# Delta rule in four groups: level masks applied by VectorE to the product P, both products of a level in two banks, and the next group's convolution inside this group's levels

## What is computed

```
proj = h @ w_in                                   # q, k (8 heads each), v, z (16 heads), width 128 each
qkv  = silu(causal_depthwise_conv(qkv, conv_w))   # 4 taps along time
q, k = l2norm(q) * 128**-0.5, l2norm(k)
decay  = exp(where(causal, gc_i - gc_j, -inf))    # gc: running sums of g
a_low  = where(strict, (k*beta) @ k.T * decay, 0)
t_inv  = inverse(eye + a_low)                     # lower triangular solve
u, w   = t_inv @ (v*beta), t_inv @ (k*beta*exp(gc))
v_new  = u - w @ state
o      = (q*exp(gc)) @ state + ((q @ k.T) * decay) @ v_new
state  = state*exp(g_last) + (k*exp(g_last-gc)).T @ v_new
out    = (rmsnorm(o) * silu(z)) @ w_o
```

## Time and profile before

| | before |
|---|---|
| median of 3 runs | 1782.59 us (1781.35 to 1784.86) |
| profiled execution, its own time | 1781.98 us |
| its span | 1780.2 us |
| PE busy | 1696.2 us, 95% |
| DVE / ACT / POOL busy | 1317.5 / 1062.6 / 177.9 us |
| DeltaNet groups in the trace | 359.7 to 735.1 us |

### The profile page before, as it was taken

The page is one execution under the profiler, slowest core; times in us unless marked ns, Lnnn a source line. Parts: engine busy times, 40 slices in busy tenths (PEclk is TensorE's granted clock), DMA queues, the critical chain, the costliest instruction groups (busy, mean ns, idle before and its releaser), DMA issues.

```text
span 1780.2 us, 23186 instructions
## 1 busy us (share of the span) xinstructions
PE 1696.2 (95%) x8998; PEld 1435.6 (81%) x8998; DVE 1317.5 (74%) x1065; ACT 1062.6 (60%) x1012; POOL 177.9 (10%) x118
## 2 busy tenths in 40 slices
PE   8899999889999988889999999999999999999996
PEld 6789998778888877768888888888888888888884
DVE  5644445494857655379889889899898898898986
ACT  4444343554545353266777777777777777777773
POOL 0100000044442617000000000000000000000000
PEclk9899999999999999989999999999999999999999
DMA  9146555242221200359999999999999999999992
GB/s 349 43 141 212 173 189 171 92 140 74 70 95 48 71 1 1 154 190 352 354 364 356 350 358 371 348 361 358 350 364 348 372 344 353 365 369 346 369 361 112
DMA packets 155422, 437.91 MB, mean 246 GB/s; under 512 B 9280, under 2 KB 40416, under 8 KB 155360
## 3 DMA queue, kind: packets, MB, share of 16 engines
q1 hardware_dynamic: 155360, 437.03, 68.3%
HBM read 435.95 MB, written 1.05 MB: 245 GB/s over the span
## 4 chain that ended last, share of the span: by engine, by line
PE 83%; DVE 10%; ACT 3%; issue 2%; DMA 1%; POOL 0%; SPq 0%; DVEq 0%; ACTq 0%; POOLq 0%
PE bank L1328 24%; PE bank L1330 24%; PE bank L1329 24%; DVE wlo L844 2%; PE bank L1708 2%; PE bank L1697 2%; PE bank L1810 1%; ACT whi L521 1%; DVE T L1097 1%; DVE TT L1119 1%; PE bank L1715 1%; DVE cvall L1036 1%; DMA raw<-in_attn_w_qkv_dram 1%; DVE wlo L1164 0%; PE bank L1833 0%
## 5 line engine op out<-in xcount | busy, mean ns | idle before, releaser
L1164 DVE TENSOR_TENSOR wlo<-raw,whi 128x2048 fp32r<-128x2048 f32 x336 | 767.6, 2291 | 111.9 <-ACT whi L745 108.8
L745 ACT CAST whi<-raw 128x2048 fp32r<-128x2048 f32 x336 | 643.4, 1916 | 245.3 <-PE bank L1330 245.3
L1328 PE MATMUL bank<-whi,xhi 128*128 128x512 f32 (+1 forms) x1584 | 576.9, 364 | 12.8 <-ACT oall L647 3.5
L1330 PE MATMUL bank<-whi,xlo 128*128 128x512 f32 (+1 forms) x1584 | 568.9, 359 | 0.0
L1329 PE MATMUL bank<-wlo,xhi 128*128 128x512 f32 (+1 forms) x1584 | 568.5, 359 | 0.0
L1328 PEld LDWEIGHTS bank<-whi,xhi 128*128 128x128 f32 x1584 | 301.1, 190 | 59.1 <-DVE wlo L844 4.1
L1330 PEld LDWEIGHTS bank<-whi,xlo 128*128 128x128 f32 x1584 | 300.9, 190 | 44.5
L1329 PEld LDWEIGHTS bank<-wlo,xhi 128*128 128x128 f32 x1584 | 301.4, 190 | 41.9
L844 DVE TENSOR_TENSOR wlo<-raw,whi 128x2048 fp32r<-128x2048 f32 x75 | 186.7, 2491 | 108.4 <-ACT whi L521 108.1
L1328 PE MATMUL bank<-whi,ehhi 128*128 128x512 f32 x448 | 178.3, 398 | 1.8 <-DVE ehlo L1179 1.8
L521 ACT CAST whi<-raw 128x2048 fp32r<-128x2048 f32 x75 | 142.9, 1905 | 60.2 <-PE bank L1330 56.0
(11 more groups left out here) (266 smaller groups left out, 1639.6 us busy)
## 6 DMA issues: line engine op xcount, KB each, us to landing
raw<-in_moe_w_gate_dram SPq DMA_DIRECT2D x112, 1024.0 KB, 6.8
raw<-in_moe_w_up_dram SPq DMA_DIRECT2D x112, 1024.0 KB, 6.8
raw<-in_moe_w_down_dram SPq DMA_DIRECT2D x112, 1024.0 KB, 6.9
raw<-in_dn_w_in_dram SPq DMA_DIRECT2D x24, 1024.0 KB, 5.3
raw<-in_ffn_w_gate_dram SPq DMA_DIRECT2D x11, 1024.0 KB, 5.8
raw<-in_ffn_w_up_dram SPq DMA_DIRECT2D x11, 1024.0 KB, 5.2
raw<-in_ffn_w_down_dram SPq DMA_DIRECT2D x11, 1024.0 KB, 4.9
raw<-in_dn_w_o_dram SPq DMA_DIRECT2D x8, 1024.0 KB, 5.2
```

The lines of the kernel that those rows point to most:

```text
L745: act.copy(slot(whi, n, SPLIT), slot(raw, n, RAW)).then_inc(hi_ready, 1)
L1164: dve.tensor_tensor(slot(wlo, n, SPLIT), slot(raw, n, RAW), slot(whi, n, SPLIT).bitcast(F32), ALU.subtract).then_inc(lo_ready, 1)
L1328: pe.matmul(ps, lhs_hi, wh, start=start, stop=False)
L1330: return pe.matmul(ps, lhs_lo, wh, start=False, stop=stop)
```

## The change

GpSimd no longer masks `A` (its 24 instructions of L473 go, `off0` and `off1` too). PE multiplies `A` itself with `TT`, and VectorE multiplies the level's mask, now transposed in the table, into P where it leaves its bank, in place of ScalarE's copy. The second product of a level and the transpose of `T` at the start go to banks 2 and 3 as well. Banks 4 and 5 so are free in the levels, and the convolution of group g+1 is done in the levels of group g: transposes in levels 1 and 4, VectorE's rounds one by one behind the subtractions, Silu in levels 4 and 6, and the decay sums behind w. Group 0's own convolution comes before the loop. `outputs_lo`, the second output block's norm and `add_outputs` move to other places of VectorE's stream; the tables of halves and panels are new (six halves ahead of the levels in groups 0 to 2, and 6, 10 and 10 in them); in group 3 two of four halves move into levels 1 and 2, and 12 activity matmuls stand for 19.

```diff
@@ scheduling tables
-        FILLED = ((2, 3, 4, 5, 6, 7, 7, 8, 9, 10, 11, 12, 12, 12), (2, 3, 4, 5, 6, 8, 9, 10, 11, 12, 13, 14, 15, 16),
-                  ..., (0, 0, 1, 2, 3, 4, 4, 4, 4, 4, 4, 4, 4, 4))
+        FILLED = ((2, 3, 4, 4, 5, 6, 7, 8, 9, 10, 11, 12), (2, 3, 4, 5, 6, 6, 8, 10, 11, 12, 14, 16),
+                  ..., (0, 0, 1, 2, 2, 2, 3, 4, 4, 4, 4, 4))
@@ gpsimd
-                pool.wait_ge(sem("A_ready"), g + 1)
-                off_diagonal(g, 1)
-                off_diagonal(g, 2)
                 scaled(g, 2, kbe, ebeta)
                 scaled(g, 2, ktail, etail)
-                for lv in range(3, LEVELS):
-                    off_diagonal(g, lv)
@@ scalar, in the levels
-                    for b in range(TB):
-                        act.wait_ge(sem("P_psum"), 2 * u + b + 1)
-                        act.copy(Pm[:, 4 * b:4 * b + 4, :], four(2 + b)).then_inc(sem("P_ready"), 1)
+                    if more and lv == 1:
+                        taps(g + 1, 0)
+                    if more and lv == 4:
+                        taps(g + 1, 1)
@@ vector, before the loop
+            for w in (2, 1, 0):
+                conv_round(0, 0, w)
             lo_panels.upto(LIST[0] + 1)
             z_scaled(0)
+            for w in (2, 1, 0):
+                conv_round(0, 1, w)
@@ vector, in the levels
+                    mask = tb_(f"level{lv}").unsqueeze(1).broadcast_to([P, GH, P])
+                    for b in range(TB):
+                        dve.wait_ge(sem("P_psum"), 2 * u + b + 1)
+                        dve.tensor_tensor(Pm[:, 4 * b:4 * b + 4, :], bank[2 + b]..., mask, ALU.mult)\
+                            .then_inc(sem("P_ready"), 1)
+                    ahead(lv)
+                    if more and lv == 6:
+                        z_scaled(g + 1)
                     for b in range(TB):
                         dve.wait_ge(sem("dTT_psum"), 2 * u + b + 1)
-                        dve.tensor_tensor(t_, t_, bank[4 + b]..., ALU.subtract)\
+                        dve.tensor_tensor(t_, t_, bank[2 + b]..., ALU.subtract)\
                             .then_inc(sem("TT_ready"), 1)
+                    if more and lv < 4:
+                        conv_round(g + 1, 0, 3 - lv)
...
@@ tensor, new functions
+            def conv_T(g, half):
+                pe.wait_ge(sem(("prj_qk_ready", "prj_v_ready")[half]), g + 1)
+                if half:
+                    pe.wait_ge(sem("conv_ready"), 2 * g + 1)
+                elif g:
+                    pe.wait_ge(sem("qdT_ready"), g)
+                ...
+            def decay_sums(g):
+                pe.wait_ge(sem("gm_ready"), g + 1)
+                pe.wait_ge(sem("conv_ready"), 2 * g + 2)
+                for b in range(TB):
+                    i = pe.matmul(bank[4 + b], tb_("ones"), gm[:, 4 * b:4 * b + 4, :], start=True, stop=True)
+                i.then_inc(sem("R_psum"), 1)
@@ tensor, before the loop
+                if i == 8:
+                    conv_T(0, 0)
+            conv_T(0, 1)
             pe.wait_ge(sem("gate_act"), 4)
+            decay_sums(0)
@@ tensor, levels and tail
-                            i = pe.matmul(bank[2 + b][...], o[:, 4 * b + h, :], TT[:, 4 * b + h, :],
+                            i = pe.matmul(bank[2 + b][...], A[:, 4 * b + h, :], TT[:, 4 * b + h, :],
                                           start=True, stop=True)
                         i.then_inc(sem("P_psum"), 1)
-                    filling(6 + lv)
+                    filling(5 + lv)
+                    if more and lv in (1, 4):
+                        conv_T(g + 1, lv // 4)
...
-                filling(13)
+                if more:
+                    decay_sums(g + 1)
```

More of the change, by code:

```diff
@@ L69, in table @@
         s = 1 << n
-        parts[f"level{n}"] = (i // (2 * s) == j // (2 * s)) & (i // s % 2 == 1) & (j // s % 2 == 0)
+        low, up = (i, j) if n == 0 else (j, i)
+        parts[f"level{n}"] = (low // (2 * s) == up // (2 * s)) & (low // s % 2 == 1) & (up // s % 2 == 0)
     at, out = 0, []
@@ L142, in trunk @@
     vb = eight("vb", 48)
-    qkT, off1 = eight("qkT", 52), eight("off1", 52)
+    qkT = eight("qkT", 52)
     A = eight("A", 56)
@@ L621, in _ @@
             act.wait_ge(sem("baT_psum"), 1)
-            act.copy(hid[0:2 * VH, 0:SEQ], bank[4][0:2 * VH, 0:SEQ]).then_inc(sem("baT_ready"), 1)
+            act.copy(hid[0:2 * VH, 0:SEQ], bank[2][0:2 * VH, 0:SEQ]).then_inc(sem("baT_ready"), 1)
             act.wait_ge(sem("rs_ready"), 3)
@@ L665, in ahead @@
                 def ahead(place):
[L666 to L673, removed]
+                    hi_panels.upto(LIST[g] + HI_AHEAD[g][place] - 1)
@@ L694, in _ @@
-                ahead(1)
                 act.wait_ge(sem("qkT_psum"), g + 1)
                 for b in range(TB):
-                    i = act.copy(qkT[:, 4 * b:4 * b + 4, :], four(b))
+                    i = act.copy(qkT[:, 4 * b:4 * b + 4, :], four(2 + b))
                 i.then_inc(sem("qkT_ready"), 1)
@@ L1110, in _ @@
                     dve.tensor_tensor(t_, eye, t_, ALU.subtract).then_inc(sem("T1_ready"), 1)
-                ahead(2)
+                if g:
+                    add_outputs(g - 1, 0, lambda b, h: 6 + b).then_inc(sem("outputs_added"), 1)
                 for lv in range(1, LEVELS):
                     u = g * (LEVELS - 1) + lv - 1
+                    mask = tb_(f"level{lv}").unsqueeze(1).broadcast_to([P, GH, P])
+                    for b in range(TB):
+                        dve.wait_ge(sem("P_psum"), 2 * u + b + 1)
+                        dve.tensor_tensor(Pm[:, 4 * b:4 * b + 4, :], bank[2 + b].rearrange("p (n f) -> p n f", n=4), mask, ALU.mult)\
+                            .then_inc(sem("P_ready"), 1)
+                    ahead(lv)
+                    if more and lv == 6:
+                        z_scaled(g + 1)
                     for b in range(TB):
@@ L1622, in filling @@
                     done[0] = max(done[0], FILLED[g][place])
-                for half in range(2):
-                    pe.wait_ge(sem(("prj_qk_ready", "prj_v_ready")[half]), g + 1)
-                    for t in range(4 * half, 4 * half + 4):
-                        src = (group_part(g), prj_v)[half]
-                        for b in range(TB):
-                            i = pe.transpose(conv_src(t)[:, b * P:(b + 1) * P], src[:, b, t % 4 * P:(t % 4 + 1) * P], ident)
-                    i.then_inc(sem("ch_psum"), 1)
+                if g:
+                    pe.wait_ge(sem("v_ready"), TB * g)
+                    pe.wait_ge(sem("S_ready"), g)
+                back(g, 0, 2)
                 filling(0)
-                if g == GROUPS - 1:
+                if not more:
                     pe.wait_ge(sem("z_scaled"), GROUPS)
-                    keep_clock(5, bank[6])
+                    keep_clock(12, bank[6])
                 if g:
```

259 lines of the change are left out of this document (128 added, 131 removed).

## The result

The changed kernel takes 1792.11 us (median of 5 runs, 1790.44 to 1793.61) against 1782.59: ratio 1.0050, 95% interval 1.0039 to 1.0061, 9.5 us slower. The forecast was 1785.1, its range ended at 1790.5. The profiled execution has a span of 1790.3 us, 10.1 over before. PE is busy 4 us more than before and GpSimd 77 less, with its masks gone.

The account below looks back on a forecast made before the run. PE, holding 83% of the chain, was taken as the bound, so only its waits count. Groups 0 to 3 gave 5.1 + 0.7 + 0.7 - 4.0 = +2.5 us, 1785.1 us; range 1777 to 1790.5.

Parts of the forecast that it names:

- Group 0, +5.1 forecast: First DeltaNet group, its own convolution ahead of the loop: ends at 457.5, 5.1 us later than before.
- The wait ahead of the decay sums: Group 0's start: PE idles 7.2 us, 360.8 to 368.0, until VectorE's convolution rounds end.
- the 2.3: Group 0's front: 2.3 us lost to the lower clock behind PE's idle stretch, taken from 1.7 or 3.0.
- Groups 1 and 2, +0.7 each forecast: Middle DeltaNet groups: front, levels and tail together 100.6 us against 99.9, 0.7 us more in each.
- the front at 26.6 us: Groups 1 and 2 ahead of the levels: 38.8 us less moved work is 25.9, plus 0.7 waiting for P.
- the pairs for `T` alone: Groups 1 and 2, VectorE's copies to `T` beside GpSimd: first pair 2.8 us, second 2.3; alone 1.4 each.
- the wait for the addition to `X`: Level 1 of groups 1 and 2: the half behind P waits 2.4 us for this addition on VectorE.
- Group 3, -4.0 forecast: Last DeltaNet group: level 3 starts at 43.4 us into the group instead of 47.4, 4.0 us less.
- my 1.5: Group 3's front: PE's 4.6 us idle stretch before `onlo` costs about 1.5 us more by the clock.
- Masks and banks at 0: All levels: VectorE's mask product adds 0 to 0.1 us a level, taken as 0; sharing one bank pair costs nothing.
- The first: Rival: clock falls at level 1 of groups 1 and 2, 1.7 us lost in each; +5.9, 1788.5; chance 0.23.
- The second: Rival: VectorE's copies to `T` wait a whole GpSimd instruction, 3.4 us a pair; +5.9, 1788.5; chance 0.12.

Follow-up runs that it names:

- a_lock: The changed kernel, but GpSimd's mask product of `E` waits until VectorE's panels ahead of `A` are made; 1788.6 us, ratio 1.0028 to the kernel before.
- a_lock2: The changed kernel, with GpSimd's mask product of `E` held until VectorE's panels are made (groups 0 to 2) and its scalings until `T` is made; 1783.9 us, ratio 1.0001.
- b_masks2: The kernel before with VectorE's level masks alone, convolution unmoved, each level's panel put between its mask and its subtraction; 1778.5 us, ratio 0.9974.
- a_clock: The changed kernel, with products of no use filling PE's four long idle stretches to hold the clock; 1789.3 us, ratio 1.0034 to the kernel before.

## Why the prediction was wrong, step by step

- **Group 0, +5.1 forecast, +6.5 measured.** The wait ahead of the decay sums was right (7.2 forecast, 6.92), and the clock fell behind it (the sums took 3.43 from start to start instead of 1.72, so 1.7 of the 2.3). P came 51.3 us behind the gate sums, where the forecast has 50.9 (397.2 against 346.26; its own terms add up to 397.0), although `A` was late by the collision (a_lock gave 1.2 back), so other terms were a little too large. In level 5 VectorE's subtraction stood behind a panel that started late since ScalarE's cast was (the row), and the level took 9.0 us instead of 7.8. So the levels took 49.5 us, not 48.3.
```profile
432.43 2.29 DVE L843 TENSOR_TENSOR wlo<-raw,whi 128x2048 fp32r<-128x2048 f32 x1 [2.31 <-ACT whi L511]
```
- **Groups 1 and 2, +0.7 each forecast, +2.4 measured.** This is the step that failed. I had the front at 26.6 us; it took 29.9. The sum took PE's moved work off before's front and added 0.7; it had no term for a wait of PE for VectorE's panel behind the transposes of q and k. I put GpSimd's collisions on the pairs for `T` alone (2.8 and 2.3), and they fell on the two panels ahead, 7.32 instead of 4.49. That cost PE 2.0 us of wait and 1.7 of clock; without them, in a_lock2, the front is 26.2. The pairs took 2.09 and 1.29. The levels took 60.5, not 62.1: the wait for the addition to `X` was 0.9, not 2.4, since the pair ahead of it ran alone. The tail was right, 11.9. Without the collision (a_lock2) these groups last 98.6, under my 100.6.
- **Group 3, -4.0 forecast, -1.3 measured.** PE did wait for `onlo`, 5.45 us instead of 4.6, and the clock stayed low for 6.9 us, where my 1.5 stands for some 3. The chain ahead was longer than summed: the reduction began 5.4 us into the group (4.9 forecast), and the scaling of q and k took 2.02 beside GpSimd's products for `EB`, against 1.23 before:
```profile
669.07 0.92 DVE L1078 TENSOR_SCALAR par<-par 128x4 f32<-128x4 f32 x1 [2.11 <-POOL par L438]
670.02 2.02 DVE L1079 TENSOR_TENSOR qk<-qk,par 128x1024 f32<-128x1024 f32 x1
671.97 1.28 DVE L1020 TENSOR_TENSOR onlo<-bank,onhi 128x512 fp32r<-128x512 f32 x2
```
  P came 28.4 us into the group, not 26.3, and level 3 at 45.6, not 43.4.
- **Masks and banks at 0: right for the masks where they stand; the bank pair has no run of its own.** All 48 mask products took 676 to 692 ns. A level without halves takes 5.17 us instead of 5.05 (705.94 to 711.11; the earlier trace rows), the 0.1 at the end of my range, and b_masks2 is faster than before with the same masks. I gave their removal from GpSimd and ScalarE no gain, and b_masks2 shows 4.5 us, with the panels' new place in the levels in it.
```profile
L1127 DVE TENSOR_TENSOR Pm<-bank,tabs x48: 676/691/692, 395.5 to 723.4; 128x512 f32<-128x512 f32 x48
```
```profile
705.94 1.95 PE L1721 MATMUL bank<-TT,A 128*128 128x128 f32 x16
...
711.11 1.06 PE L1721 MATMUL bank<-TT,A 128*128 128x128 f32 x8
```
- **The rivals.** The first (the clock falls at level 1 of groups 1 and 2) had the price right, 1.7 us a group, and the place wrong: it fell in the front, behind a wait that the rival doesn't have. In these groups it came at level 1 only in a_clock. The second (a whole instruction of GpSimd ahead of each of VectorE's) is what happened, on other instructions than I named. The Trainium skill (SBUF — State Buffer, SBUF: two separate sides) says that whichever starts first holds the shared port for its whole instruction; the trace agrees, since GpSimd's product began at 469.52 and the panel, begun at 469.76, ended 2.14 us after that product's end, close to the 2.28 that it takes alone.

## What to carry to other kernels

When work is moved away from an engine, list what its remaining instructions now stand beside, not only what they cost: here GpSimd's mask product came to stand beside two panels in a row, and its scalings, which no longer wait for `A`, right behind it. Two waits that hold early, unneeded instructions back until their neighbours are done lengthened nothing that PE needs and returned 8.7 us (1.0050 to 1.0001). Two causes in one chain can each give little alone (0.3 and 1.2 us, and 4.0 together): repair both before calling either useless.

## What the runs showed of the hardware

A VectorE instruction that reads a bank kept its length beside GpSimd. In the changed kernel no mask product stood beside it, but in a_lock2 the first ones of groups 0 to 2 did, and took 680 to 692 ns all the same:
```profile
482.84 2.04 POOL L466 TENSOR_TENSOR kbe<-qk,par 128x512 f32<-128x512 f32 x2 [6.96 <-DVE T L1123]
483.87 1.28 DVE L1131 TENSOR_TENSOR Pm<-bank,tabs 128x512 f32<-128x512 f32 x2
```
One of VectorE's with two tiles took up to nearly twice its length, a panel 4.27 us instead of 2.28, and GpSimd's own waited likewise, the half of `kbe` 3.08, three times its 1.03:
```profile
469.76 4.27 DVE L843 TENSOR_TENSOR wlo<-raw,whi 128x2048 fp32r<-128x2048 f32 x1
471.85 3.08 POOL L466 TENSOR_TENSOR kbe<-qk,par 128x512 f32<-128x512 f32 x1
```
And filling a wait of 3.3 us with products of no use did not save the clock: in a_clock it fell later in the group, for the same 3.4 us. Why it fell there, and why group 3 of a_lock had more of it, is open.
